# Stick-breaking attention: mask products grouped, the next pair's scores issued ahead of the sums, two sum products instead of three, and half of the output projection issued inside the last pair

## What is computed

```python
def stick_breaking_attention(h, w_in, w_out):
    qkv = (h @ w_in).reshape(b, s, 3, SB_HEADS, SB_HEAD_DIM)
    q, k, v = qkv[:, :, 0], qkv[:, :, 1], qkv[:, :, 2]
    def block(args):                      # 128 queries
        z = jnp.einsum('bqhd,bkhd->bhqk', qb, k).astype(jnp.float32) * scale
        mask = k_idx[None, :] < q_idx[:, None]
        sp = jnp.where(mask, jax.nn.softplus(z), 0.0)
        tail = lax.cumsum(sp, axis=sp.ndim - 1, reverse=True) - sp
        log_a = jax.nn.log_sigmoid(z) - tail
        a = jnp.where(mask, jnp.exp(log_a), 0.0).astype(v.dtype)
        return jnp.einsum('bhqk,bkhd->bqhd', a, v)
    return merge_blocks(lax.map(block, ...)) @ w_out
```

## Time and profile before

| | before |
|---|---|
| median of 3 runs | 2883.1 us (2882.57 to 2890.91) |
| span of the profiled execution | 2876.3 us |
| median less that span | 6.8 us |
| PE busy over the span | 2505.8 us, 87% |
| mean granted clock of PE | 0.954 |
| from scores(0) to the end of the layer's output projection | 236.6 to 353.7 us: 117 us, 4% of the span |

### The profile page before, as it was taken

The page is one execution under the profiler, slowest core; times in us unless marked ns, Lnnn a source line. Parts: engine busy times, 40 slices in busy tenths (PEclk is TensorE's granted clock), DMA queues, the critical chain, the costliest instruction groups (busy, mean ns, idle before and its releaser), DMA issues.

```text
span 2876.3 us, 35601 instructions
## 1 busy us (share of the span) xinstructions
PE 2505.8 (87%) x12218; PEld 1786.6 (62%) x12218; DVE 1729.8 (60%) x3508; ACT 1190.2 (41%) x2574; POOL 964.3 (34%) x745
## 2 busy tenths in 40 slices
PE   8999899999989999996888778778886988777777
PEld 8988799999869988975444333333763444333334
DVE  5552355655555555785666767765566666676663
ACT  4346544443464356553333333333462333233333
POOL 0015400000330027665444333343544444433443
PEclk9999999999999999998999998999998999999999
DMA  6543255555315544436999999997439999999994
GB/s 212 191 169 118 96 195 185 174 185 184 133 63 201 182 149 152 134 118 264 416 411 418 421 421 419 420 413 322 137 104 375 412 417 413 420 420 417 417 414 185
DMA packets 141958, 783.51 MB, mean 272 GB/s; under 512 B 15872, under 2 KB 16384, under 8 KB 76288
## 3 DMA queue, kind: packets, MB, share of 16 engines
q0 software_dynamic: 73728, 536.90, 45.0%
q1 hardware_dynamic: 65360, 237.44, 24.4%
q10 hardware_dynamic: 2736, 7.46, 0.8%
HBM read 780.69 MB, written 1.05 MB: 272 GB/s over the span
## 4 chain that ended last, share of the span: by engine, by line
PE 47%; DMA 23%; DVE 10%; issue 7%; ACT 6%; POOL 6%; ACTq 0%; POOLq 0%; DVEq 0%; SPq 0%
DMA arena<-experts,arena 23%; PE ps L473 12%; PE ps L474 12%; PE ps L475 12%; PE ps L991 5%; PE ps L994 5%; POOL ring_lo L316 3%; DVE arena L2110 2%; POOL arena L2213 2%; ACT row L1468 2%; ACT arena L1461 1%; ACT L1459 1%; POOL rs L2192 1%; DVE arena L2002 1%; DVE hT_lo L1664 0%
## 5 line engine op out<-in xcount | busy, mean ns | idle before, releaser
L2110 DVE SCALAR_TENSOR_TENSOR arena<-arena,ps 128x1024 f32<-128x1024 f32 x512 | 618.4, 1220 | 432.5 <-DMA arena<-experts,arena 417.2
L991 PE MATMUL ps<-arena,row 128*128 128x512 f32 x1024 | 584.5, 655 | 279.6 <-ACT row L1468 269.7
L2213 POOL DMA_INDIRECT arena<-experts,arena x512 | 484.2, 946 | 686.1 <-PE ps L994 486.9
L473 PE MATMUL ps<-hT_hi,ring_hi 128*128 128x256 f32 x2056 | 588.9, 286 | 11.2 <-DVE hT_lo L1664 8.5
L474 PE MATMUL ps<-hT_lo,ring_hi 128*128 128x256 f32 x2056 | 582.6, 283 | 0.0
L475 PE MATMUL ps<-hT_hi,ring_lo 128*128 128x256 f32 x2056 | 582.3, 283 | 0.0
L994 PE MATMUL ps<-arena,row 128*128 128x512 f32 x1024 | 562.2, 632 | 0.0
L316 POOL TENSOR_TENSOR ring_lo<-ring,ring_hi 128x1024 fp32r<-128x1024 f32 x182 | 451.1, 2491 | 313.2 <-ACT ring_hi L310 238.4
L991 PEld LDWEIGHTS ps<-arena,row 128*128 128x128 f32 x1024 | 199.9, 205 | 571.2 <-ACT row L1468 344.0
L310 ACT ACTIVATE ring_hi<-ring 128x1024 fp32r<-128x1024 f32 x448 | 462.8, 1058 | 108.9 <-PE ps L475 94.7
L473 PEld LDWEIGHTS ps<-hT_hi,ring_hi 128*128 128x128 f32 x2056 | 393.9, 192 | 19.2 <-DVE ring_lo L316 6.1
(11 more groups left out here) (278 smaller groups left out, 2995.5 us busy)
## 6 DMA issues: line engine op xcount, KB each, us to landing
ring<-stream SPq DMA_DIRECT2D x448, 512.0 KB, 4.2
arena<-experts,arena POOLq DMA_INDIRECT x512
row<-rows_in ACTq DMA_DIRECT2D x11, 512.0 KB, 4.4
x<-x_in SPq DMA_DIRECT2D x1, 1024.0 KB, 5.0
out<-arena SPq DMA_DIRECT2D x2, 512.0 KB, 2.6
arena<-cols_in ACTq DMA_DIRECT2D x3, 256.0 KB, 7.6
cols<-cols_in SPq DMA_DIRECT2D x1, 425.5 KB, 5.6
arena<-cols_in ACTq DMA_DIRECT2D x1, 320.0 KB, 3.0
```

The costliest lines, as they stand in the source:

```text
L473: pe.matmul(dst, a[0], b[0], start=start, stop=False)
L991: lower = pe.matmul(ps[:, 2 * tb, :], diag, v[:, 0:HALF], start=first, stop=end)
L2110: last = dve.scalar_tensor_tensor(u, u, 1.0, h, ALU.mult, ALU.mult, accum_out=R["a"][:, n % 2, k:k + 1])
L2213: pool.indirect_dma_start(R["held"][:, g % HELD, :], None, experts, bass.IndirectOffsetOnAxis(ap=idx[:, n % 2, k:k + 1], axis=0))\
```

## The change

Five edits, all in stick-breaking.

1. `scores(j)` issues the masks of both heads first, then the 256-column products of both heads, then the 128-column ones.
2. `sums(j)` issues two products a head (384 and 128 columns) instead of three (256, 128, 128). The columns are 512 in both.
3. In the loop PE issues scores(j+1) ahead of sums(j). What frees the scores' bank is now `sb_sp` and no longer `sb_t`; for that DVE copies z before it makes softplus, as soon as ACT has made |z| (a new semaphore `sb_az`).
4. ACT loads exp's table right behind ln (`preload_act_table`), and makes both of a turn's high parts before it waits for `sb_t`, and in the last turns one more.
5. Of the output projection PE issues blocks 24 to 27's products for the first 128 tokens around values(6), ahead of sums(7), and those for the other tokens behind sums(7), ahead of values(7). DVE makes the low parts of blocks 29 and 31 (POOL did).

```diff
+LATE_BY_DVE = {AT["sb_out"] + 5, AT["sb_out"] + 7}
...
                     else:
-                        pe.wait_ge(of("sb_t"), j - 1)
+                        pe.wait_ge(of("sb_sp"), j - 1)
                     pe.wait_ge(of("sb_qk"), j + 1)
+                    z = [ps[:, 2 * (j % 2) + e, :] for e in range(2)]
+                    h = [slice(64 * e, 64 * e + 64) for e in range(2)]
                     for e in range(2):
-                        z, h = ps[:, 2 * (j % 2) + e, :], slice(64 * e, 64 * e + 64)
-                        pe.matmul(z[:, 0:384], R["mask"][:, 0:P], R["mask"][:, P:4 * P], start=True, stop=False)
-                        pe.matmul(z[:, 0:T], k_[h, 0:P], q[h, :], start=False, stop=False)
-                        last = pe.matmul(z[:, T:T + P], k_[h, P:T], q[h, P:T], start=False, stop=True)
+                        pe.matmul(z[e][:, 0:384], R["mask"][:, 0:P], R["mask"][:, P:4 * P], start=True, stop=False)
+                    for e in range(2):
+                        pe.matmul(z[e][:, 0:T], k_[h[e], 0:P], q[h[e], :], start=False, stop=False)
+                    for e in range(2):
+                        last = pe.matmul(z[e][:, T:T + P], k_[h[e], P:T], q[h[e], P:T], start=False, stop=True)
                     last.then_inc(of("sb_s"), 1)
...
-                        pe.matmul(r[:, 0:T], R["own"][:, 3, :], sp_[:, 0:T], start=True, stop=False)
-                        pe.matmul(r[:, P:T], col("ones"), sp_[:, T:T + P], start=False, stop=True)
-                        last = pe.matmul(r[:, T:T + P], R["own"][:, 3, :], sp_[:, T:T + P], start=True, stop=True)
+                        pe.matmul(r[:, 0:384], R["own"][:, 3, :], sp_[:, 0:384], start=True, stop=False)
+                        last = pe.matmul(r[:, P:T], col("ones"), sp_[:, T:T + P], start=False, stop=True)
...
+                out, tiles = AT["sb_out"], parts_of(R["oT"])
+
+                def out_of_first(ks):
+                    for k in ks:
+                        wait_split(pe, out + k)
+                        pe.wait_ge(of("sb_o"), k + 1)
+                        for half in range(2):
+                            by_rows(ps[:, half, :], tiles(k, 0), out + k, half, k == 0, False)
+
+                def out_of_second(ks):
+                    for k in ks:
+                        for half in range(2):
+                            last = by_rows(ps[:, 2 + half, :], tiles(k, 1), out + k, half, k == 0, False)
+                        last.then_inc(used, 1)
+
                 split_row_blocks(base, KD, entering=NORM_OF["sb"])
                 project(0)
                 scores(0)
-                for j in range(pairs):
-                    if j + 1 < pairs:
-                        project(j + 1)
+                for j in range(pairs - 1):
+                    project(j + 1)
                     if j >= 1:
                         values(j - 1)
+                    scores(j + 1)
                     sums(j)
-                    if j + 1 < pairs:
-                        scores(j + 1)
+                out_of_first(range(2))
+                values(pairs - 2)
+                out_of_first(range(2, TAIL))
+                sums(pairs - 1)
+                out_of_second(range(TAIL))
                 values(pairs - 1)
-                projected(AT["sb_out"], KD, parts_of(R["oT"]), lambda k: pe.wait_ge(of("sb_o"), k + 1))
+                last_row_blocks(out, KD, tiles, lambda k: pe.wait_ge(of("sb_o"), k + 1))
...
-                    link(act.activation(R["az"], z, ACT.Abs))
+                    act.activation(R["az"], z, ACT.Abs).then_inc(of("sb_az"), 1)
+                    act.wait_ge(of("sb_az"), j + 1)
                     link(act.activation(R["ez"], R["az"], ACT.Exp, scale=-1.0))
                     act.activation(R["lz"], R["ez"], ACT.Ln, bias=1.0).then_inc(of("sb_l"), 1)
+                    act.preload_act_table(ACT.Exp)
                     ahead(KD + 2 * j + 4)
                     if j + 1 < pairs:
                         take(j + 1)
+                        ahead(KD + 2 * j + 5)
+                    if j + 2 == pairs:
+                        ahead(KD + 2 * j + 6)
                     act.wait_ge(of("sb_t"), j + 1)
                     if j >= 1:
                         act.wait_ge(of("sb_av"), j)
                     act.activation(R["a"], R["t"], ACT.Exp).then_inc(of("sb_a"), 1)
-                    ahead(KD + 2 * j + 5)
+                    if j + 2 == pairs:
+                        ahead(KD + 2 * j + 7)
...
+                    dve.wait_ge(of("sb_az"), j + 1)
+                    link(dve.tensor_copy(R["z"], ps[:, 2 * (j % 2):2 * (j % 2) + 2, 0:384]))
                     dve.wait_ge(of("sb_l"), j + 1)
...
-                    link(dve.tensor_copy(R["z"], ps[:, 2 * (j % 2):2 * (j % 2) + 2, 0:384]))
...
+                make_lo(dve, AT["sb_out"] + 5)
                 dve.wait_ge(of("sb_av"), pairs)
                 split_out(R["oT"], pairs - 1, ps[:, 7, 0:T], of("sb_o"))
+                make_lo(dve, AT["sb_out"] + 7)
```

More of the change, by code:

```diff
@@ L89, in split_blocks @@
             who = "dve" if (name.startswith("ffn") and AT[name] + n not in SECONDS
-                            or AT[name] + n in FIRST_BY_DVE) else "pool"
+                            or AT[name] + n in FIRST_BY_DVE or AT[name] + n in LATE_BY_DVE) else "pool"
             of_block[AT[name] + n] = (len(of_block), who, made[who])
@@ L1181, in take @@
                     act.activation(R["k"][:, j % 2], ps[:, 6, T:2 * T], ACT.Copy).then_inc(of("sb_qk"), 1)
+                begun = [SLOTS]
                 def ahead(b):
-                    if b < 3 * KD + SLOTS:
+                    if b == begun[0] and b < 3 * KD + SLOTS:
+                        begun[0] += 1
                         make_hi(act, base + b)
@@ L2200, in lows @@
                 for b in range(first + turns * SLOTS, end):
-                    make_lo(pool, b)
+                    if b not in LATE_BY_DVE:
+                        make_lo(pool, b)
             def expert_rows(l, at):
```

## The result

The changed kernel is slower: 2891.7 us (median of 7 runs, 2888.1 to 2896.3) against 2882.2 (2879.8 to 2890.9), a ratio of 1.0027 with a 95% interval of 1.0014 to 1.0040. The profiled execution has a span of 2886.5 us (2876.3 before). 2879.1 us was predicted, with a range up to 2886.

A forecast was written before the change was run, and what follows sets the result against it. PE was taken to bound the loop, busy 11.21 of 11.35 us a turn. Entry -0.7, six turns +4.6 and tail -7.8 gave -3.9, rounded 4.0: span 2872.3, plus 6.8 makes 2879.1 us, range 2869 to 2886.

The forecast's parts named there:

- Scores 1.37 us: PE, each pair: masks first and both heads' products side by side take 0.18 + 0.34 + 0.85 = 1.37 us, before 2.42.
- The sums' edit: PE, each pair's sums: two products a head instead of three were given nothing, at most 0.1 us a pair.
- The circle: Loop: scores(j+1) wait through ACT for sums(j), now behind scores(j); 12.10 us a turn against 9.95 of PE's work, 2.15 idle.
- The price of the preload in it: ACT, in the loop's circle: exp's table load behind ln adds 1.30 us a turn.
- The tail: From the start of scores(7) to the layer's end: 30.8 us instead of 38.6, so -7.8 us.
- the clock in the loop: Rival, 7%, the slower case: behind each turn's 2.15 us idle, scores and sums at 1.2 GHz, 3.1 us more; 2901.
- the signs: Profile after: masks 12.1 us apart, PE idle about 2.1 ahead, scores 1.4, clock 1.00 throughout, layer's end some 4 us earlier.
- The bound before: Loop of the kernel before: PE was taken as the bound, busy 11.21 of 11.35 us a turn at full clock.
- the sum of the prediction: Whole layer: entry -0.7, six turns +4.6, tail -7.8, together -3.9 us.

The follow-up runs named there:

- the run with the sums first: The changed kernel with sums(j) issued ahead of scores(j+1) again, the rest of the change kept: 2867.2 us, 0.9944 of the kernel before.
- the run with the gap filled: The changed kernel with 8 products nobody reads issued behind values(j-1), where PE waits for the copies of q and k: 2881.9 us, 0.9991 of before.
- masks alone: The kernel before with only the new order inside scores (both masks first, then both heads' products): 2886.2 us, 1.0005 of before.
- order alone: The kernel before with only scores(j+1) ahead of sums(j) and DVE's copy of z ahead of softplus: 2907.4 us, 1.0081 of before.

## Why the prediction was wrong, point by point

- **Scores 1.37 us**: right to the hundredth at full clock (236.59 to 237.96); the two heads do run beside each other. The sums' edit is worth 0.02 us: in the run with the sums first they take 1.76 (286.73 to 288.49), against 1.78. PE's turn there is 9.89, and 9.95 was the sum.
- **The circle**: right. 12.10 us was the sum, 12.04 and 12.11 are what it measures at full clock, and the idle time was put at 2.15 and is 2.11 to 2.18 (2.30 ahead of pair 1). Its place and releaser are those named. The price of the preload in it was put at 1.3 a turn; taking it out made the turn 10.68, 1.43 less than 12.11.
- **The tail**: 30.8 us was the sum. It is 32.4 (326.62 to 358.99), and the difference of 1.6 is scores(7) and sums(6) at half clock: from scores(7) to the next layer's transposes the run with the gap filled has 32.78 us and the changed kernel 34.34. The waits in it are 0.20 for POOL and 0.65 for DVE, as two rows of the changed kernel show:

```profile
336.98 0.50 PE L474 MATMUL ps<-ring_hi,oT_at 128*128 128x512 f32 x1 [0.20 <-POOL ring_lo L317]
...
339.29 0.91 PE L621 MATMUL ps<-arena 128*128 128x384 f32 x2 [0.65 <-DVE arena L1759]
```

- **The step that failed is the clock in the loop.** The sum has no term for its fall, and the signs name "the clock 1.00 throughout the layer". The fall stood among the rivals as the slower case, with the right place and 7%. It was discounted because one window of another layer showed PE busy 7.15 of 12.00 us at clock 1.00, a larger idle share than the new turn's. That argument compared shares. PE's idle time in that window is in pieces, and the longest is 1.20 us:

```profile
2089.41 0.87 PE L688 MATMUL ps<-cols,arena 128*128 128x128 f32 x6 [1.20 <-DVE arena L1804]
```

  So the window said nothing of a single gap of 2.15 us. In the changed kernel the clock fell behind six gaps of seven, of 2.11 to 2.18 us each, at a share of 9.9 busy in 12.0. The Trainium skill (TensorE: Matmul & The Clock Gate, HAM oscillation), which was cited against the change, tells of a clock that falls anew with each recurring wait. The trace of after agrees in six turns of seven, though the waits of the page's kernel are longer than these.
- **Its price** was set too high in the rival (3.1 us a turn, all of scores and sums at half clock) and is 1.6: the second sum product, from 303.19, takes 0.81 us, as it does at full clock. Six such falls are 9.4 us, and with them the sum of the prediction would have been -3.9 + 9.4 = +5.5 us in the layer, where 5.4 is measured, and 2888.5 us in all.
- **The bound before** was read as PE, and that is wrong. The wait of 0.34 us for POOL's low part, which the prediction lists, was the mark of a closed circle of 11.34 us: shortening PE's work by 1.05 in masks alone gained 0.06, and putting the scores into the circle in order alone made it 13.76. It did not harm the sum, because the change opens that circle and the prediction took the 0.34 off.
- What isn't explained: the medians differ by 9.5 us (by the ratio 7.8), the layer by 5.4. The rest is within the interval of the ratio, and the layers outside vary by 13 us between profiled executions of the same code there (2757.3 to 2770.3). But it leans one way: of the eleven kernels timed against the one before, ten have a median 0.8 to 4.9 us above what their stretch gives against 119.0, and only order alone lies below. The stretch of before comes from one execution, and its old tail isn't steady: behind scores(7) the three profiled kernels that keep it and the loop's old order have 39.05, 40.58 and 41.89 us, depending on when the clock came back. So 119.0, and with it the 5.4, may be off by some 1.5 us (an estimate from these three). No run settles whether a part of the rest is real.

## What to carry to other kernels

When work is issued earlier on one engine, follow every wait of the moved work back through the others until it comes round to itself, and add up that circle. Here PE's shorter turn (9.9 us) was the bound only in the two kernels with the sums first. In the others one of three circles through ACT, DVE and POOL was, of 10.7 to 13.8 us, depending on what stood ahead of what on ACT and PE. A small wait that comes in every turn, like the 0.34 us before, can be the mark of such a circle, even where PE's busy share is 99%. A gap that recurs on PE is to be priced with the clock in it: filling it with products that nobody reads gave 9.4 us back in this layer, and opening the circle 24.

## What the runs showed of the hardware

- The clock's fall doesn't go by the length of one gap alone. It stayed at 1.00 with one gap a turn of 0.76, 1.09 and 1.43 us. In the changed kernel it stayed behind the first gap, of 2.30 us, and fell behind each of the six of 2.11 to 2.18 that followed. With the order alone it fell behind the first four gaps, of 2.42 to 2.50 us, and stayed behind the last two, of 2.50.
- With the falling clock the changed kernel's turns came out alike to a hundredth, 13.66 or 13.67 us, five in a row. With the order alone they didn't: 15.04, 15.14 and 15.28.
- ACT_TABLE_LOAD holds up what stands behind it on ACT, whether that needs a table or not, and costs somewhat more than its own length. In the changed kernel the high part starts 2.16 us behind ln with the preload between them, and without it, in the second pair of rows, 0.75 us behind, since two neighbouring ACTIVATEs overlap by 0.1:

```profile
295.39 0.85 ACT L1225 ACTIVATE arena<-arena 128x768 f32<-128x768 f32 x1
297.55 1.06 ACT L311 ACTIVATE ring_hi<-ring 128x1024 fp32r<-128x1024 f32 x1
```

```profile
296.11 0.85 ACT L1225 ACTIVATE arena<-arena 128x768 f32<-128x768 f32 x1
296.86 1.04 ACT L311 ACTIVATE ring_hi<-ring 128x1024 fp32r<-128x1024 f32 x1
```

  That is 1.41 us for a load of 1.28, and it is what the turn lost (12.11 less 10.68 is 1.43). The Trainium skill (ScalarE: Activation LUTs, What ACT_TABLE_LOAD costs) gives 2.66 us for a switch with its drain; no row here shows the drain, and the measurement decides.
